# First two tiles behind a layer norm computed from the un-normalised input

## The chip, the cores and the metric

One core of a Trainium2 chip runs the whole program. The metric is device time in microseconds from start to end of one execution, the median of three.

## What is computed

Two model blocks at T = 512 tokens and D = 1024. The second block is, in order: sparse attention, layer norm, gated feed-forward, layer norm, HGRN mixer, layer norm, gated feed-forward, layer norm. What the change touches is this:

```python
for layer in range(2):
    mix = dsa_mixer(h, ...) if layer == 0 else hgrn2_mixer(h, ...)
    h = layer_norm(ALPHA * h + mix, ln_g[layer, 0], ln_b[layer, 0])
    ffn = (silu(h @ w_gate[layer]) * (h @ w_up[layer])) @ w_down[layer]
    h = layer_norm(ALPHA * h + ffn, ln_g[layer, 1], ln_b[layer, 1])

def layer_norm(x, g, b):        # mean and variance over the 1024 features of a token
    return (x - mu) * rsqrt(var + 1e-5) * g + b
```

Three of these norms are followed by a matrix product on their result: behind the attention's output projection (`wo`) comes the first feed-forward (`ffn0`), behind `ffn0` comes the HGRN stage, behind HGRN's output projection (`ho`) comes `ffn1`. The fourth norm is stored.

## The kernel before

Activations lie transposed: 128 features on the partitions, 512 tokens along the free axis, eight such tiles (KT = 8) in `c.x`. Weights stream from HBM as slabs of 128 x 1024 numbers, each slab holding the eight 128 x 128 blocks (k = 0 to 7) of one output tile, into a ring of four buffers. float32 precision is kept by splitting each number into a high part (type fp32r) and the rest: ACT casts a slab (`cast_slab`, L145), DVE subtracts (`split_slab`, L150), and each product of a weight block with an activation tile is three matmuls (`product`, L176 to L178) of 128x128 weights and 512 columns. An output tile is therefore 24 matmuls in one PSUM bank. Two slabs (three in the HGRN stage) are held split at a time; PE waits for the split, ACT's next cast waits for PE to be done with the slab that it replaces. All ordering is by semaphores written by hand; within an engine the program order holds.

The program is a list of stages with a barrier of all engines between them. At a boundary with a layer norm this happens:

- `stage_project` (L1879) or the second half of `stage_ffn` (L2003) makes output tile m = 0 to 7. DVE adds it to the residual in `c.x` (L1935 or L2137), ACT squares it (`scalar_square`, L1730), and DVE and POOL keep running sums of x and of its squares over tiles 0 to 6 (L1747, L1738).
- When the last product is done, `Norm.tensor` (L1750) sums over the partitions on PE with single-column matmuls (L1758): the running sums first, then tile 7 and its square. DVE and ACT make mean, variance and the inverse root (`Norm.vector` L1790, `Norm.scalar` L1781), PE spreads the two resulting rows over all partitions (L1777) into banks 2 and 3. Between the sums and the spread PE runs `warm` (L184), matmuls whose results nobody reads. Meanwhile ACT casts and DVE splits three slabs of the next stage. Then the stage ends.
- In the next stage `Apply` normalises in place: for each k DVE multiplies and adds (L1831, L1834), ACT makes the high part with g and b (L1845) and the full value (L1847), POOL subtracts (L1853). PE runs `warm` again (ten calls) and then `first_pair` (L209): output tiles 0 and 1 advance together, k by k, each k as `Apply` delivers it. Then tiles 2 and 3, then the loop.

In the feed-forward stage the slabs alternate gate and up; four slabs are a turn. ACT applies Silu to the gate tile (L2081), DVE multiplies by the up tile (L2115), both parts of the result go to `hid` (L2084, L2118). In the HGRN stage (L2660) four slabs make one head (forget gate, value, query, output gate, tiles u = 4h to 4h+3), computed in banks 0 and 1 in turn; ACT's `taken` (L2845) moves each tile out of its bank. PE runs `dense(4)`, `turned(0)` (transposes of head 0 through banks 2 and 3), `dense(5)`, `inner(0)`, `update(0)`, `dense(6)`, `outer(0)` (L2781), and so on.

Of the kernel before, what the change touches and what calls it, by code (L numbers as in the profile page):

```python
# [13 lines left out]
P = 128  # L14
# [53 lines left out]
class Ctx:  # L68
# [58 lines left out]
    def place_third(self, n, tile):  # L127

        at = self.bigr[:, tile:tile + 4, :].rearrange("p a b -> p (a b)")
        self.third = {n: at.rearrange("p (a k c) -> p a k c", a=2, k=KT)}  # L130
# [9 lines left out]
    def cast_slab(self, act, n, i=0):  # L140

        act.wait_ge(self.slab_ready[n % RING], 16 * (n // RING + 1) + i * 16)
        if n >= self.held and n not in self.third:
            act.wait_ge(self.slab_done, n - self.held + 1 + i * RING)
        act.activation(self.place(n)[:, 0, :, :], self.ring[:, n % RING, :, :], ACT.Copy).then_inc(self.slab_cast, 1)  # L145
# [1566 lines left out]

class Norm:
# [4 lines left out]
    def __init__(self, c, tag, squares, at, kind, g, b=None, eps=1):  # L1718
        self.squares = squares
# [7 lines left out]

    def scalar_square(self, act, added, m):
        wait_tile(act, added, m)
        act.activation(self.squares[:, m, :], self.c.x[:, m, :], ACT.Square).then_inc(self.sq_out, 1)  # L1730

    def pool(self, pool):

        for m in range(1, KT - 1):
            pool.wait_ge(self.sq_out, m + 1)
            if m > 1:
                pool.wait_ge(self.sq_added, m - 1)
            pool.tensor_tensor(self.acc[:, 1, :], self.squares[:, 0, :] if m == 1 else self.acc[:, 1, :],  # L1738
                               self.squares[:, m, :], ALU.add).then_inc(self.sq_added, 1)
# [10 lines left out]
    def tensor(self, pe, added):  # L1750

        c = self.c
        one = con(c, "ones")[:, 0:1]

        def sums(bank, x, first):
            for q in range(QT):
                for half in HALVES:
                    mm = pe.matmul(bank[half, q:q + 1], x[:, q * P:(q + 1) * P][:, half], one, start=first and q == 0,  # L1758
                                   stop=not first, skip_group_check=True)
            return mm  # L1760

        wait_tile(pe, added, KT - 3)
        if self.kind == "ln":
            pe.wait_ge(self.x_added, KT - 2)
            sums(c.bank[0], self.acc[:, 0, :], True)
        pe.wait_ge(self.sq_added, KT - 2)
        sums(c.bank[1], self.acc[:, 1, :], True)
        if self.kind == "ln":
            pe.wait_ge(added, KT)
            sums(c.bank[0], c.x[:, KT - 1, :], False).then_inc(self.sums, 1)  # L1770
        pe.wait_ge(self.sq_out, KT)
        sums(c.bank[1], self.squares[:, KT - 1, :], False).then_inc(self.sums, 1)
        warm(c, pe, c.bank[4], 4)
        pe.wait_ge(self.small, 1)
        for j, row in enumerate((4, 5)[:2 if self.kind == "ln" else 1]):
            for q in range(QT):
                mm = pe.matmul(c.bank[2 + j][:, q * P:(q + 1) * P], self.st[:, row, q:q + 1].to_broadcast([P, P]),  # L1777
# [3 lines left out]
    def scalar(self, act, ahead=None):  # L1781
# [4 lines left out]
        if ahead:  # L1786
# [3 lines left out]
    def vector(self, dve, ahead=None):  # L1790
# [3 lines left out]
        if self.kind == "ln":  # L1794
            ch.link(dve.tensor_scalar(st[:, 0, :], c.bank[0][:, 0:QT], 1.0 / D, None, ALU.mult))
            ch.link(dve.tensor_tensor(st[:, 1, :], st[:, 0, :], st[:, 0, :], ALU.mult))
            dve.wait_ge(self.sums, 2)
            dve.scalar_tensor_tensor(st[:, 2, :], c.bank[1][:, 0:QT], 1.0 / D, st[:, 1, :], ALU.mult, ALU.subtract)\
               .then_inc(self.root, 1)
        else:  # L1800
            dve.tensor_scalar(st[:, 2, :], c.bank[1][:, 0:QT], 1.0 / D, None, ALU.mult).then_inc(self.root, 1)
# [6 lines left out]
        if ahead:  # L1808
# [4 lines left out]
class Apply:  # L1813
# [3 lines left out]
    def __init__(self, c, tag, parts=True):  # L1817
        self.c, self.n, self.parts = c, c.norm, parts
# [3 lines left out]
    def vector(self, dve):  # L1822
# [6 lines left out]
        for k in range(KT + 1):  # L1829
            if k < KT:  # L1830
                dve.tensor_tensor(c.x[:, k, :], c.x[:, k, :], c.bank[2][:, :], ALU.mult).then_inc(self.scaled, 1)  # L1831
            if k >= 1:
                dve.wait_ge(self.scaled, k)
                dve.tensor_tensor(c.x[:, k - 1, :], c.x[:, k - 1, :], c.bank[3][:, :], ALU.add).then_inc(self.normed, 1)  # L1834

    def scalar(self, act):
        c, n = self.c, self.n
        for k in range(KT):
# [5 lines left out]
            if self.parts:  # L1844
                act.activation(c.hr[:, k, :], c.x[:, k, :], ACT.Identity, **affine).then_inc(self.cast, 1)  # L1845
# [25 lines left out]
FFN_THIRD, DSA_THIRD = 20, 24  # L1871
# [7 lines left out]
def stage_project(c, tag, slab, alpha, norm, next_parts, src=None, begun=0, parts=(1,)):  # L1879
# [3 lines left out]
    norm = Norm(c, tag, c.big, 10, *norm)  # L1883
    c.place_parts(*parts)
    c.norm = norm
    yp = parts_of(c, f"{tag}_y", c.y if src is None else src)

    def after():

        c.place_parts(*next_parts(c))  # L1890
        c.place_third(slab + KT + 2, FFN_THIRD)
        return slab + KT

    with nc.Block() as block:
# [17 lines left out]
        def _(act):  # L1912
# [3 lines left out]
            for m in range(KT):  # L1916
                if m + PARTS < KT:
                    c.cast_slab(act, slab + m + PARTS)
                norm.scalar_square(act, added, m)
            norm.scalar(act, after())  # L1920
            c.place_parts(*parts)
# [6 lines left out]
        def _(dve):  # L1928
            if not begun:
                open_dense(c, yp, slab, dve=dve)  # L1930
            for m in range(KT):
                if m + PARTS < KT:
                    c.split_slab(dve, slab + m + PARTS)
# [6 lines left out]
def stage_out(c):  # L1940
# [9 lines left out]
    def next_stage():  # L1950

        c.place_parts(*dsa_parts(c))
        c.place_third(slab + slabs + 2, DSA_THIRD)
# [49 lines left out]
def stage_ffn(c, layer):  # L2003
# [6 lines left out]
    xp = Apply(c, f"{tag}x")  # L2010
    norm = Norm(c, tag, c.h, 27, "ln", ("ln_g", (2 * layer + 1) * KT), ("ln_b2", (2 * layer + 1) * KT))
# [3 lines left out]
    c.place_parts(*ffn_parts(c))  # L2015
    c.norm = norm
    down_made = c.sem(f"{tag}_down_made")
# [11 lines left out]
    with nc.Block() as block:  # L2029
# [6 lines left out]
        def _(pe):  # L2036

            def gate_up(u, i):
                c.slab_wait(pe, gu + u, i)
                for k in range(KT):  # L2040
                    mm = product(pe, c.bank[u][:, :], c.slab_parts(gu + u, k), xp.tile(k), k == 0, k == KT - 1)
                mm.then_inc(c.slab_done, 1)

            c.place_third(gu + 2, FFN_THIRD)
# [5 lines left out]
            c.third = {}  # L2050
# [7 lines left out]
            for n in range(KT * FT):  # L2058
# [3 lines left out]
                if m == 0:  # L2062
                    pe.wait_ge(hidden_out, j + 1)
                mm = product(pe, down_bank(m), c.slab_parts(dn + n // KT, n % KT), (hid[:, j, :], hid_lo[:, j, :]),
# [8 lines left out]
        def _(act):  # L2073
            def turn(i, first):

                for u in range(2):
                    c.slab_done_wait(act, gu + 2 * u, i)
                    if u or not first:
                        c.cast_slab(act, gu + 2 * u + PARTS, i)
# [3 lines left out]
                    act.wait_ge(prod_out, i * 2 + (u + 1))  # L2083
                    act.activation(hid[:, i * 2 + u, :], prod[:, u, :], ACT.Copy).then_inc(cast_out, 1)  # L2084
# [3 lines left out]
            turn(0, True)  # L2088
            with act.Fori(1, FT // 2) as i:
                turn(i, False)  # L2090
            act.preload_act_table(ACT.Sqrt)
            for s in range(FT):
                if s + PARTS < FT:
                    c.cast_slab(act, dn + s + PARTS)
                if s in down_end:
                    norm.scalar_square(act, added, down_end.index(s))
            norm.scalar(act, after())
            c.place_parts(*ffn_parts(c))
# [7 lines left out]
        def _(dve):  # L2106
            def turn(i, first):

                for u in range(2):
                    for v in range(2):  # L2110
                        if u or v or not first:
                            c.split_slab(dve, gu + 2 * u + v + PARTS, i)
# [3 lines left out]

                    dve.wait_ge(cast_out, i * 2 + (u + 1))
                    dve.tensor_tensor(hid_lo[:, i * 2 + u, :], prod[:, u, :], hid[:, i * 2 + u, :].bitcast(F32), ALU.subtract)\  # L2118
                       .then_inc(hidden_out, 1)

            xp.vector(dve)
            turn(0, True)
            with dve.Fori(1, FT // 2) as i:
                turn(i, False)
            made = 0
            for s in range(FT):
                if s + PARTS < FT:
                    c.split_slab(dve, dn + s + PARTS)
                if s in down_end:

                    m = down_end.index(s)
# [1129 lines left out]
```

## Time and profile before

| | us |
|---|---|
| median of 3 runs | 1902.44 |
| lowest, highest | 1901.03, 1903.01 |
| the profiled execution | 1900.69 |
| its span, first to last instruction | 1898.8 |
| PE busy | 1811.3 (95%) |
| DVE busy | 897.9 (47%) |
| ACT busy | 781.5 (41%) |
| POOL busy | 246.2 (13%) |
| mean granted TensorE clock | 0.985 |

The page has the busy time of each engine over the whole span and in 40 slices, the granted TensorE clock in the same slices, and the groups of instructions by line. A busy PE is not always a useful one: L184 (`warm`) counts as busy. The four boundaries with a layer norm lie near 818, 1192, 1503 and 1878 us of the span; the first three are those that the change touches.

### The profile page before, as it was taken

What the parts mean: (1) busy time and instruction counts of PE and PEld (TensorE: products, weight loads), DVE (VectorE), ACT (ScalarE), POOL (GpSimd) and SP (SyncE); (2) the same over time, 40 slices, a digit from 0 to 9 for tenths busy, and PEclk for the clock granted to TensorE, in tenths of its full rate; (3) what the DMA queues carried; (4) which work ended last, traced back from release to release, by engine and by line L of the source; (5) the groups of instructions that cost most, each with busy time, mean ns of one, the idle gap of its engine ahead of it and who ended that gap; (6) DMA issues with size and microseconds to landing.
All of it is one profiled execution on the core that took longest, in us unless ns stands there. A gap on an engine that the chain in (4) does not pass through costs nothing. (4 is left out here: it accounts for less than half of the span.)

```text
span 1898.8 us, 31549 instructions
## 1 busy us (share of the span) xinstructions
PE 1811.3 (95%) x12642; PEld 1419.9 (75%) x12642; DVE 897.9 (47%) x1644; ACT 781.5 (41%) x1341; POOL 246.2 (13%) x205
## 2 busy tenths in 40 slices
PE   6999999899899899999999999999998999999996
PEld 5776666576775666778888888788887778888885
DVE  2673554555557796343333323654554533333223
ACT  4543444455443445342323222765563333222222
POOL 3011232000125000120000000322320210000000
PEclk9999999899999899999999999999999999999998
DMA  5231101200121000213323233222221222332331
GB/s 185 89 92 66 35 25 36 84 23 12 45 74 45 1 1 1 75 64 95 99 99 91 97 100 98 66 87 69 77 67 31 92 75 91 99 99 94 95 100 45
DMA packets 38488, 134.00 MB, mean 71 GB/s; under 512 B 4896, under 2 KB 5344, under 8 KB 38112
## 3 DMA queue, kind: packets, MB, share of 16 engines
q1 hardware_dynamic: 37504, 130.07, 21.5%
q8 instruction: 87, 1.43, 0.3%
q10 hardware_dynamic: 864, 2.23, 0.3%
q14 instruction: 33, 0.27, 0.0%
HBM read 129.40 MB, written 2.10 MB: 69 GB/s over the span
## 5 line engine op out<-in xcount | busy, mean ns | idle before, releaser
L150 DVE TENSOR_TENSOR big_parts<-ring,big_parts 128x1024 fp32r<-128x1024 f32 x181 | 226.7, 1256 | 532.6 <-ACT big_parts L145 531.2
L176 PE MATMUL bank<-h_parts,big_parts 128*128 128x512 f32 (+1 forms) x1072 | 423.9, 395 | 8.3 <-DVE big_parts L150 4.9
L177 PE MATMUL bank<-y_parts,big_parts 128*128 128x512 f32 (+1 forms) x1072 | 417.2, 389 | 0.0
L178 PE MATMUL bank<-h_parts,big_parts 128*128 128x512 f32 (+1 forms) x1072 | 417.2, 389 | 0.0
L145 ACT ACTIVATE big_parts<-ring 128x1024 fp32r<-128x1024 f32 x181 | 191.3, 1060 | 382.9 <-PE bank L178 380.1
L176 PEld LDWEIGHTS bank<-h_parts,big_parts 128*128 128x128 f32 x1072 | 201.9, 188 | 59.0 <-POOL y_parts L1853 6.8
L178 PEld LDWEIGHTS bank<-h_parts,big_parts 128*128 128x128 f32 x1072 | 201.8, 188 | 42.0
L177 PEld LDWEIGHTS bank<-y_parts,big_parts 128*128 128x128 f32 x1072 | 202.0, 188 | 39.4
L176 PE MATMUL bank<-big_parts 128*128 128x512 f32 x352 | 136.9, 389 | 0.0
L177 PE MATMUL bank<-work_parts,big_parts 128*128 128x512 f32 x352 | 136.9, 389 | 0.0
L178 PE MATMUL bank<-big_parts 128*128 128x512 f32 x352 | 136.9, 389 | 0.0
L1235 ACT ACTIVATE work<-work 128x256 f32<-128x256 f32 (+4 forms) x128 | 67.1, 524 | 110.9 <-DVE work L1257 110.5
L184 PE MATMUL bank<-cst 128*128 128x256 f32 x356 | 101.1, 413 | 8.2 <-PEq L92 8.2
L176 PE MATMUL bank<-h_parts,work_parts 128*128 128x512 f32 x232 | 93.9, 405 | 1.2 <-PEq L92 0.8
L184 PEld LDWEIGHTS bank<-cst 128*128 128x128 f32 x356 | 70.8, 207 | 28.1 <-issue 15.5
L1257 DVE CUSTOM_DVE_ANT_0 work<-bank,big 128x256 f32<-128x256 f32 (+4 forms) x128 | 56.8, 444 | 73.2 <-PE bank L1204 63.7
L178 PE MATMUL bank<-h_parts,work_parts 128*128 128x512 f32 x232 | 90.5, 390 | 0.0
L177 PE MATMUL bank<-y_parts,work_parts 128*128 128x512 f32 x232 | 90.4, 390 | 0.0
L832 PE MATMUL bank<-x,ring 128*128 128x512 f32 x176 | 85.7, 610 | 0.2 <-ACT big L1031 0.2
L150 DVE TENSOR_TENSOR work_parts<-ring,work_parts 128x1024 fp32r<-128x1024 f32 x37 | 46.2, 1252 | 76.9 <-ACT work_parts L145 76.8
L177 PEld LDWEIGHTS bank<-work_parts,big_parts 128*128 128x128 f32 x352 | 66.1, 188 | 13.8
L176 PEld LDWEIGHTS bank<-big_parts 128*128 128x128 f32 x352 | 66.1, 188 | 13.7
(399 smaller groups left out, 2696.1 us busy)
## 6 DMA issues: line engine op xcount, KB each, us to landing
ring<-in_wstream SPq DMA_DIRECT2D x229, 512.0 KB, 3.6
x<-in_xt SPq DMA_DIRECT2D x8, 512.0 KB, 6.7
out_t<-x SPq DMA_DIRECT2D x8, 256.0 KB, 2.0
work<-in_memt ACTq DMA_DIRECT2D x1, 1024.0 KB, 14.2
y<-in_cw SPq DMA_DIRECT2D x1, 1024.0 KB, 5.0
cst<-in_cst ACTq DMA_DIRECT2D x1, 768.0 KB, 7.9
cos<-in_reset SPq DMA_DIRECT2D x2, 256.0 KB, 6.8
big<-work SPq DMA_DIRECT2D x4, 128.0 KB, 4.5
```

What stands on the lines that cost most here:

```text
L145: act.activation(self.place(n)[:, 0, :, :], self.ring[:, n % RING, :, :], ACT.Copy).then_inc(self.slab_cast, 1)
L150: dve.tensor_tensor(self.place(n)[:, 1, :, :], self.ring[:, n % RING, :, :], self.place(n)[:, 0, :, :].bitcast(F32), ALU.subtract).then_in ...
L176: pe.matmul(out, w[0], x[0], start=start, stop=False, skip_group_check=True)
L177: pe.matmul(out, w[0], x[1], start=False, stop=False, skip_group_check=True)
L178: return pe.matmul(out, w[1], x[0], start=False, stop=stop, skip_group_check=True)
L184: pe.matmul(bank[:, 0:2 * P], con(c, "ident"), c.cst[:, 0:2, :], start=True, stop=True)
L832: mm = pe.matmul(c.bank[DENSE_BANK][:, :], c.raw_slab(n, k), c.x[:, k, :], start=k == 0, stop=k == KT - 1)
L1235: act.activation(e, e, ACT.Exp, bias=self.low[:, n:n + 1], scale=-1.0, accum_out=self.den[:, n:n + 1])\
L1257: dve.tensor_tensor_reduce(self.weights(n), self.c.bank[self.SCORES[n % 3]][:, 0:u.keys], u.mask, -self.scale, 3e38, ALU.add, ALU.min, sel ...
```

## The change

At the first three boundaries output tiles 0 and 1 of the next stage no longer wait for the norm. With W a weight block and r, mu the inverse deviation and mean of a token, W(g(x - mu)r + b) = r W(gx) - (mu r) W g + W b. A new class `Raw` holds g times x in two parts, made tile by tile while the stage before still runs. PE multiplies with these; the two vectors W g and W b come from 16 small matmuls on the unsplit slabs in the ring (two columns each). k = 0 and 1 of both tiles are done among the statistics, k = 2 to 7 at the start of the next stage (`raw_products`). Then ACT copies both banks out (`copy_opened`) after its whole share of `Apply`, and DVE multiplies by r and adds (`open_tile`); W b goes in as a bias of the first use. Tile 2 now runs alone, k by k with `Apply`.

What moves with it: the running sums are reduced before the last product (last two k-steps in `ffn0`) rather than behind it (`early`); all `warm` calls at these boundaries go; the slabs of tiles 0 and 1 are cast and split inside the loop over m, to places of their own, and behind the norm only two slabs are (tiles 2 and 3); sums and spread use other banks. In HGRN tiles 2 and 3 use banks 2 and 3, so `turned(0)` waits for tile_out 4 instead of 2, the slab of tile 4 is split behind `open_tile`, and `decays` comes behind that. In `ffn0` the squares have two buffers instead of eight.

```diff
+class Raw:
+    def scalar(self, act, k):
+        act.activation(self.hi[:, k, :], self.c.x[:, k, :], ACT.Copy, scale=vec(self.c, self.g[0], self.g[1] + k)).then_inc(self.cast, 1)
+    def vector(self, dve, k):
+        dve.wait_ge(self.cast, k + 1)
+        dve.scalar_tensor_tensor(self.lo[:, k, :], self.c.x[:, k, :], vec(...), self.hi[:, k, :].bitcast(F32), ALU.mult, ALU.subtract)...
+    def columns(self, pe):
+        for u in range(2):
+            c.raw_wait(pe, self.slab + u)
+            for k in range(KT):
+                mm = pe.matmul(c.bank[2][:, 2 * u:2 * u + 2], c.raw_slab(self.slab + u, k), c.vecs[:, g:b + 1:b - g], ...)
+        mm.then_inc(self.cols_made, 1)
+    def begin(self, pe, k):
+        pe.wait_ge(self.split, k + 1)
+        if k == 0:
+            for u in range(2):
+                self.c.slab_wait(pe, self.slab + u)
+        self.product(pe, k)
...
     def scalar_square(self, act, added, m):
...
+        if self.raw:
+            self.raw.scalar(act, m)
...
     def tensor(self, pe, added):
+        if self.raw:
+            self.raw.begin(pe, 0)
+        else:
+            self.early(pe, added)
         if self.kind == "ln":
             pe.wait_ge(added, KT)
...
-        warm(c, pe, c.bank[4], 4)
+        if self.raw:
+            for k in range(1, Raw.BEGUN):
+                self.raw.begin(pe, k)
+        else:
+            warm(c, pe, c.bank[4], 4)
         pe.wait_ge(self.small, 1)
...
         ins.then_inc(self.small, 1)
-        if ahead:
+        if self.raw:
+            self.raw.vector(dve, KT - 1)
+            self.raw.columns_out(dve)
+            for n in range(2, 4):
+                c.split_slab(dve, ahead + n)
...
+    def open_tile(self, dve, u):
+        dve.wait_ge(self.opened_raw, u + 1)
+        dve.tensor_tensor(self.opened[u], self.opened[u], n.spread_banks[0][:, :], ALU.mult).then_inc(self.opened_half, 1)
+        dve.wait_ge(self.opened_half, u + 1)
+        dve.scalar_tensor_tensor(self.opened[u], n.spread_banks[1][:, :], self.raw.columns_at[:, 2 * u:2 * u + 1], self.opened[u],
+                                 ALU.mult, ALU.add).then_inc(self.opened_out, 1)
...
 stage_project, tensor:
+                    if m == KT - 1 and k == KT - 1:
+                        norm.early(pe, added)
...
 stage_ffn, tensor:
-            warm(c, pe, c.bank[4], 10)
-            first_pair(c, pe, gu, xp)
-            xp.wait_banks(pe)
-            for u in range(2, 4):
-                gate_up(u, 0)
+            xp.raw_products(pe)
+            onward()
+            gate_up(2, 0, True)
+            gate_up(3, 0)
...
 stage_ffn, scalar:
             xp.scalar(act)
-            turn(0, True)
+            xp.copy_opened(act)
+            xp.opened_wait(act, 0)
+            act.activation(silu[:, 0, :], xp.opened[0], ACT.Silu, bias=xp.opened_bias(0)).then_inc(silu_out, 1)
+            high(0, 0)
+            turn(0, (1,))
...
 stage_hgrn, tensor:
-                pe.wait_ge(tile_out, 4 * h + 2)
+                pe.wait_ge(tile_out, 4 * h + 2 if h else 4)
...
 stage_hgrn, scalar and vector:
             xp.scalar(act)
+            xp.copy_opened(act)
+            c.cast_slab(act, n0 + 4)
...
             xp.vector(dve)
+            for u in range(2):
+                xp.open_tile(dve, u)
+            c.split_slab(dve, n0 + 4)
             decays()
```

## Rows read from the trace of the kernel before

**Rows 1.** Page: busy us, share of the span and instructions by engine.

```profile
PE 1811.3 (95%) x12642; PEld 1419.9 (75%) x12642; DVE 897.9 (47%) x1644; ACT 781.5 (41%) x1341; POOL 246.2 (13%) x205
```

**Rows 2.** Timeline, PE, first boundary: start us, length us, instruction, idle before.

```profile
818.49 1.10 PE L1758 MATMUL bank<-cst,work 128*64 128x1 f32 x32
819.45 0.61 PE L1758 MATMUL bank<-cst,x 128*64 128x1 f32 x16
820.01 0.63 PE L1758 MATMUL bank<-cst,big 128*64 128x1 f32 x16
820.57 3.06 PE L184 MATMUL bank<-cst 128*128 128x256 f32 x8
823.43 2.58 PE L1777 MATMUL bank<-cst,work 128*128 128x128 f32 x16
826.80 4.56 PE L184 MATMUL bank<-cst 128*128 128x256 f32 x20 [0.79 <-PEq L92]
831.88 0.47 PE L176 MATMUL bank<-h_parts,big_parts 128*128 128x512 f32 x1 [0.52 <-POOL y_parts L1853]
```

**Rows 3.** Timeline, DVE, the same stretch.

```profile
818.60 0.69 DVE L1935 SCALAR_TENSOR_TENSOR x<-x,bank 128x512 f32<-128x512 f32 x1 [4.02 <-PE bank L178]
...
821.50 0.16 DVE L1806 SCALAR_TENSOR_TENSOR work<-work 128x4 f32<-128x4 f32 x1
822.23 3.50 DVE L150 TENSOR_TENSOR big_parts<-ring,big_parts 128x1024 fp32r<-128x1024 f32 x3 [0.57 <-ACT big_parts L145]
```

**Rows 4.** Timeline, ACT, the same stretch.

```profile
829.57 0.82 ACT L1847 ACTIVATE x<-x,vecs 128x512 f32<-128x512 f32 x1
...
831.13 0.81 ACT L1847 ACTIVATE x<-x,vecs 128x512 f32<-128x512 f32 x1
```

**Rows 5.** Window: length, busy of PE to POOL, granted clock, DMA, GB/s.

```profile
822.00:823.00 1.00, 1.00 (x3) 0.73 (x3) 0.77 (x1) 1.00 (x2) 0.00 (x0) 0.50 0.00 0
```

**Rows 6.** Timeline, PE: third gate-up tile, first tile of the loop.

```profile
844.21 0.39 PE L176 MATMUL bank<-h_parts,big_parts 128*128 128x512 f32 x1
...
855.10 0.39 PE L176 MATMUL bank<-h_parts,big_parts 128*128 128x512 f32 x1
```

**Rows 7.** Timeline, PE, second boundary and the first head of the HGRN stage.

```profile
1192.47 1.10 PE L1758 MATMUL bank<-cst,work 128*64 128x1 f32 x32
...
1194.55 1.99 PE L184 MATMUL bank<-cst 128*128 128x256 f32 x8
1196.38 1.95 PE L1777 MATMUL bank<-cst,work 128*128 128x128 f32 x16
...
1200.55 4.55 PE L184 MATMUL bank<-cst 128*128 128x256 f32 x20 [2.22 <-PEq L92]
...
1236.70 0.48 PE L176 MATMUL bank<-h_parts,big_parts 128*128 128x512 f32 x1
...
1251.30 1.05 PE L2789 MATMUL bank<-work 128*128 128x128 f32 x8
```

**Rows 8.** Timeline, PE, third boundary.

```profile
1503.30 1.10 PE L1758 MATMUL bank<-cst,work 128*64 128x1 f32 x32
...
1511.31 4.55 PE L184 MATMUL bank<-cst 128*128 128x256 f32 x20 [2.16 <-PEq L92]
```

**Rows 9.** Timeline, ACT, first head of the HGRN stage.

```profile
1216.35 0.22 ACT L2864 ACTIVATE work<-work 128x16 f32<-128x16 f32 x1
1216.58 1.28 ACT L2848 ACT_TABLE_LOAD   x1
...
1218.37 1.05 ACT L145 ACTIVATE big_parts<-ring 128x1024 fp32r<-128x1024 f32 x1
...
1231.04 0.59 ACT L2848 ACTIVATE big<-bank 128x512 f32<-128x512 f32 x1
```

**Rows 10.** Timeline, PE, start of the second project stage.

```profile
1467.92 0.79 PE L176 MATMUL bank<-h_parts,big_parts 128*128 128x512 f32 x1 [4.87 <-DVE big_parts L150]
...
1473.21 0.43 PE L176 MATMUL bank<-h_parts,big_parts 128*128 128x512 f32 x1
```

More of the change, by code:

```diff
@@ L125, in place_parts, with place_apart @@
         self.third = {}
-    def place_third(self, n, tile):
-        at = self.bigr[:, tile:tile + 4, :].rearrange("p a b -> p (a b)")
-        self.third = {n: at.rearrange("p (a k c) -> p a k c", a=2, k=KT)}
+    def place_apart(self, tiles):
+        self.third = {n: self.bigr[:, tile:tile + 4, :].rearrange("p a b -> p (a b)").rearrange("p (a k c) -> p a k c", a=2, k=KT)
+                      for n, tile in tiles.items()}
     def place(self, n):
@@ L1726, in __init__, with square @@
         self.st = wk(c, 0, 8, QT)
+    def square(self, m):
+        return self.squares[:, m % self.squares.shape[1], :]
     def scalar_square(self, act, added, m):
         wait_tile(act, added, m)
-        act.activation(self.squares[:, m, :], self.c.x[:, m, :], ACT.Square).then_inc(self.sq_out, 1)
+        held = self.squares.shape[1]
+        if m >= held:
+            act.wait_ge(self.sq_added, max(1, m - held))
+        act.activation(self.square(m), self.c.x[:, m, :], ACT.Square).then_inc(self.sq_out, 1)
+        if self.raw:
+            self.raw.scalar(act, m)
     def pool(self, pool):
@@ L1748, in vector_add, with column_sums, early @@
                               ALU.add).then_inc(self.x_added, 1)
[L1750 to L1760, printed above, removed]
+    def column_sums(self, pe, bank, x, first):
+        for q in range(QT):
+            for half in HALVES:
+                mm = pe.matmul(bank[half, q:q + 1], x[:, q * P:(q + 1) * P][:, half], con(self.c, "ones")[:, 0:1],
+                               start=first and q == 0, stop=not first, skip_group_check=True)
+        return mm
+    def early(self, pe, added):
         wait_tile(pe, added, KT - 3)
@@ L1807, in vector @@
         ins.then_inc(self.small, 1)
-        if ahead:
+        if self.raw:
+            self.raw.vector(dve, KT - 1)
+            self.raw.columns_out(dve)
+            for n in range(2, 4):
+                c.split_slab(dve, ahead + n)
+        elif ahead:
             for n in range(3):
@@ L1882, in stage_project, with here @@
     added = c.sem(f"{tag}_added")
-    norm = Norm(c, tag, c.big, 10, *norm)
-    c.place_parts(*parts)
+    ahead = slab + KT
+    raw = Raw(c, tag, ahead, *norm[1:], wkr(c, T, KT, T), wkr(c, 12 * T, KT, T))
+    norm = Norm(c, tag, c.big, 10, *norm, raw=raw)
     c.norm = norm
+    def here():
+        c.place_parts(*parts)
+        c.place_apart({ahead: FFN_APART[0], ahead + 1: FFN_APART[1]})
+    here()
     yp = parts_of(c, f"{tag}_y", c.y if src is None else src)
@@ L1890, in after @@
         c.place_parts(*next_parts(c))
-        c.place_third(slab + KT + 2, FFN_THIRD)
-        return slab + KT
+        return ahead
     with nc.Block() as block:
@@ L2063, in _ @@
                     pe.wait_ge(hidden_out, j + 1)
+                if raw and m == KT - 1 and j == FT - 2:
+                    norm.early(pe, added)
                 mm = product(pe, down_bank(m), c.slab_parts(dn + n // KT, n % KT), (hid[:, j, :], hid_lo[:, j, :]),
@@ L2106, in _, with low, turn @@
         def _(dve):
-            def turn(i, first):
-                for u in range(2):
+            def low(i, u):
+                dve.wait_ge(cast_out, i * 2 + (u + 1))
+                dve.tensor_tensor(hid_lo[:, i * 2 + u, :], prod[:, u, :], hid[:, i * 2 + u, :].bitcast(F32), ALU.subtract)\
+                   .then_inc(hidden_out, 1)
+            def turn(i, us):
+                for u in us:
                     for v in range(2):
-                        if u or v or not first:
-                            c.split_slab(dve, gu + 2 * u + v + PARTS, i)
+                        c.split_slab(dve, gu + 2 * u + v + PARTS, i)
                     dve.wait_ge(silu_out, i * 2 + (u + 1))
@@ L2953, in split @@
             def split(u):
-                if u < ahead:
+                if 4 < u < ahead:
                     c.split_slab(dve, n0 + u)
@@ L3041, in _ @@
             xp.vector(dve)
+            for u in range(2):
+                xp.open_tile(dve, u)
+            c.split_slab(dve, n0 + 4)
             decays()
```

194 lines of the change are left out of this document (137 added, 57 removed).

## The prediction, as recorded before the run

> **What bounds the kernel now.** I read the page first: PE is busy 95% of the span, every other engine under half [rows 1]. So the time is PE's, and a change counts by the PE time it takes out, plus any gap it opens. Then the timeline of PE around a layer norm, because the busy share hides something there. The first boundary's last product is done at 818.49 and the next product starts at 831.88 [rows 2]. In these 13.4 us PE does 2.1 us of single-column sums and 2.6 us of spreading; the two L184 rows, 3.06 and 4.56 us, are work that nobody reads. The reader is to see that PE is "busy" and waits for DVE, ACT and POOL. The DVE timeline shows the chain: last addition 0.11 us after the last product, the small statistics done at 821.66 (L1806), three splits until 825.73, barrier, next stage at 826.80 [rows 2, 3]. There PE waits 5.08 us for the first k of `Apply`; from then on ACT sets the pace, two activations in 1.56 us per k (829.57 to 831.13) [rows 4]. A pair of tiles needs 6 matmuls per k. Two whole tiles, 48 matmuls, go from 844.21 to 855.10: 0.227 us each, 5.44 us a tile [rows 6], so a k of the pair is 1.36 us of work in a 1.56 us slot.
>
> All times below are full clock first. E is the end of the last product before the norm, S the start of the next stage, E' and S' the same after the change.
>
> **From the last product to the next stage.** *Moved ahead of E:* the reduction of the running sums, 0.96 us (819.45 - 818.49) [rows 2]. Before, DVE's addition of tile 7 hid it; now it lies bare on PE. *Added ahead of E:* 16 matmuls of 128x128 float32 weights and two columns. The trace has no such shape. Lower bound: the sums with 64-wide weights and one column, 0.96 / 32 = 0.030 us, doubled for the width, 1.0 us in all. Upper bound: the spread's 128x128 weights with 128 columns, 16 in 1.95 us at full clock [rows 7]. I take 1.9, since its weight block is the same and a load of weights does not shrink with the columns. So E' = E + 2.9 (2.0 to 2.9).
>
> *Behind E':* k = 0 of two tiles, six matmuls, 1.36 us, covers the addition. Then sums of tile 7 and its square, 0.56 us each (820.01 - 819.45) [rows 2]: the last begins at 1.92. From the start of that group to the end of L1806 it was 1.65 us (821.66 - 820.01) [rows 2, 3], so the statistics are there at E' + 3.57. PE does k = 1 until 3.84 and the spread in at most 2.58 [rows 2]: 6.4. DVE has the low part of g x tile 7 (0.69, as L1935), a small copy (0.16) and two splits of 3.50 / 3 = 1.17 us [rows 3]: E' + 6.85 with the small gaps. DVE stays the last, and the barrier adds 0.84 (the smallest gap in these rows is 0.79 [rows 2]): S' = E' + 7.7. Before, S - E was 8.31, 8.08 and 8.01 us at the three boundaries [rows 2, 7, 8]. With 2.9 before E', S' is later than S by 2.3, 2.5 and 2.6 us. One split fewer on DVE is about eaten by k = 0 ahead of the sums and the two DVE steps.
>
> The additional work inside the loop over m (ACT's g x, 0.6 to 0.8 us per tile; DVE's low part 0.69) I cost at nothing: a tile gives 5.44 us, ACT then has about 2.5 and DVE about 3.1 us of work in it. If that cover went, PE would wait for the split of slab m + 2; the smallest margin I find is 1.5 us, at the second tile of the `wo` stage. The squares' two buffers cost nothing either: POOL needs 1.3 us and tiles are 15 us apart there.
>
> **The feed-forward stages (two).** Before: the loop's first tile starts 28.3 us behind S (855.10 - 826.80) [rows 2, 6]. After: k = 2 to 7 of the pair, 36 matmuls, 8.2 us, need nothing. Tile 2 can start k at S' + 5.08 + 1.556 k, the last at 15.97 (+ 0.6 of doubt), and three matmuls take 0.68: its end is S' + 16.6. Tile 3 ends at S' + 22.05. Gain within the stage 6.25 us; what is late next is `Apply`, tile 2 has 5.44 us of work in the 8.4 that are left. Net 6.25 - 2.3 = 3.95 and 6.25 - 2.6 = 3.65. The new end of the pair does not bind: ACT ends `Apply` at S' + 14.5, copies two banks (1.1), DVE opens both tiles (4 x 0.65) by 17.8, the first product of gate and up and its parts are there at 20, the slab of the loop's first tile is split at 21.5, 0.5 us before PE asks for it. That is thin; each us that ACT is later is a us of PE.
>
> **The HGRN stage.** It is different, because ACT moves every tile. Before, ACT takes tile 3 at 1231.04 (ends 1231.63), S + 31.1, and its Exp for the gate bounds runs at S + 15.8 [rows 7, 9]. After: copies until S' + 15.6, DVE opens until 17.8, splits slab 4 until 18.9, begins `decays`, and ACT's Exp comes at 19.4: 3.6 us later. From there the chain keeps its table loads (1.28 each) and loses two casts (1.05 each) and half a us of waiting [rows 9]: tile 3 is out at S' + 32.4. `turned(0)` now wants just that. PE is done with `dense(4)` at S' + 27.5 and stands 4.9 us. `dense(5)` starts at S' + 33.2, before at S + 36.15 [rows 7]; with S' = S + 2.5 that is 0.5 us gained. Head 0's states on DVE hold `outer(0)` at S' + 48.1; before it ran at S + 50.75 = S' + 48.2 [rows 7]. So this boundary gives nothing: 0.1 us.
>
> **The clock.** After 2.1 us of single-column sums at the first boundary the granted clock was 0.50, the lower of the two levels (1.2 instead of 2.4 GHz), and eight L184 matmuls took 3.06 instead of 1.99 us [rows 2, 5, 7]; at the second boundary the same sums did no harm. It was hidden behind DVE. After the change the stretch of narrow matmuls is 2.9 us and what follows, k = 0, leads to the sums, on the path. Bounds: 0, or 1.36 us (k = 0 at half rate) and a little more, up to 1.7. I take 1.3 at two boundaries of three: 2.6. The gap of 4.9 us in HGRN has a twin: at 1467.92 PE had stood 4.87 us, and the matmuls from there to 1473.21 came at half rate [rows 10], 5.3 us for 2.65 of work. Price 0 to 2.6; I take 1.5, of which 0.5 hides behind head 0's states: 1.0.
>
> The Trainium skill, "TensorE: Matmul & The Clock Gate", section "Why this matters for your kernels", speaks against removing filler matmuls: it says to keep the engine continuously busy and that gaps between bursts send it back to the slow clock. By it all four places would pay and tile 2, at 44% duty, might too; that is the rival "slower".
>
> **Sum.** 3.95 + 3.65 + 0.1 - 1.0 - 2.6 = 4.1 us. Against the profiled execution's own 1900.69 (span 1898.8 and 1.9 around it) that gives 1896.6; the median of the runs is 1.75 above that execution, so 1898.3.
>
> **The rivals.**
> - *The clock holds.* Single-column sums cost no clock at two of three boundaries, so it may hold. Then 7.6 us less: 1894.8; with the columns at their lower bound 2.7 more, 1892.1. Against it: the narrow stretch is longer than the one behind which it fell.
> - *ACT's chain is the bound.* The change doesn't do what it says where ACT is last: openings and copies come after all of `Apply`. If ACT and DVE are 1 us later than summed at each boundary (margin 0.5 in the feed-forward, none in HGRN), 2.5 us go: 1901, no change that can be told.
> - *Slower: the clock falls wherever PE is thinned.* In tile 2's stretch each k is 0.68 us in 1.56. At half rate a k still fits (1.36), but tile 3 behind it doubles. At 2.65 us a place [rows 10], the seven places (three norms, three tiles 2, one gap) cost 18.5 against the 7.7 gained: 1913. It decides from three such places on. For it: rows 5 and 10. Against it: the pair's other stretches are full.
>
> **How the numbers follow.** Forecast 0.45 (own range 1896 to 1901), clock holds 0.25, ACT's chain 0.18, slower 0.12. The range 1893 to 1904.5 leaves out the far ends of the first and last rival. 0.2% is 3.8 us, about what a measurement of this kernel can tell; faster means under 1898.6. That is all of "clock holds" and a bit over half of the forecast: 0.50; slower by as much 0.11; within 0.39.
>
> **What would show it.** Columns: the new group's 16 matmuls last 1.0 or 1.9 us. S' - E' near 7.7. First tile of the feed-forward loop at S' + 22, `dense(5)` at S' + 33, PE's longest wait there for ACT, near 4.9 us. Granted clock 0.5 in a few us behind E'. Wrong would be: PE waiting for a split at the loop's start, a wait for `added` in the loop over m, or half clock in tile 3.

## The result and the profile after

The changed kernel is slower. Six runs of each on one chip:

| | before | after |
|---|---|---|
| median, us | 1902.31 | 1908.66 |
| lowest, highest | 1901.03, 1905.36 | 1907.88, 1910.73 |
| ratio, 95% interval | | 1.0036 [1.0026, 1.0046] |
| span of the profiled execution | 1898.8 | 1906.7 |
| mean granted clock | 0.985 | 0.976 |

From the page of after, busy time by engine, the line that answers to [rows 1]:

```profile
PE 1814.9 (95%) x12654; PEld 1424.9 (75%) x12654; DVE 919.3 (48%) x1683; ACT 798.9 (42%) x1371; POOL 245.1 (13%) x205
```

The difference is a third of a per cent, but the interval lies clear of 1. Two executions further down, far slower than the others of the same kernel (2268 us for the last one, 5389 for before), are left out of the medians.

PE is no less busy than before, although all filler matmuls at three boundaries are gone.

Timeline of PE in after, first boundary (start us, length us, instruction, idle before), which answers to [rows 2]:

```profile
819.77 1.10 PE L1810 MATMUL bank<-cst,work 128*64 128x1 f32 x32
820.80 4.92 PE L1738 MATMUL bank<-vecs,ring 128*128 128x2 f32 x32
825.59 0.77 PE L176 MATMUL bank<-h_parts,work_parts 128*128 128x512 f32 x1
...
827.01 0.63 PE L176 MATMUL bank<-work_parts,big_parts 128*128 128x512 f32 x1
...
835.73 0.47 PE L176 MATMUL bank<-work_parts,big_parts 128*128 128x512 f32 x1 [1.47 <-PEq L92]
```

The early sums (L1810) and the columns (L1738) stand ahead of the last product, which begins at 825.59. At 827.01 starts k = 0 of the new pair (the place that the prediction calls E'), and the next stage starts at 835.73 (S'). The same rows at the other two boundaries answer to [rows 7, 8]:

```profile
1193.89 1.10 PE L1810 MATMUL bank<-cst,work 128*64 128x1 f32 x32
1194.92 3.73 PE L1738 MATMUL bank<-vecs,ring 128*128 128x2 f32 x32
1198.51 0.73 PE L176 MATMUL bank<-big_parts 128*128 128x512 f32 x1
...
1201.17 0.63 PE L176 MATMUL bank<-y_parts,big_parts 128*128 128x512 f32 x1
...
1209.07 0.47 PE L176 MATMUL bank<-y_parts,big_parts 128*128 128x512 f32 x1 [1.57 <-PEq L92]
...
1508.51 1.10 PE L1810 MATMUL bank<-cst,work 128*64 128x1 f32 x32
1509.54 4.24 PE L1738 MATMUL bank<-vecs,ring 128*128 128x2 f32 x32
1513.64 0.77 PE L176 MATMUL bank<-h_parts,big_parts 128*128 128x512 f32 x1
...
1515.07 0.63 PE L176 MATMUL bank<-work_parts,big_parts 128*128 128x512 f32 x1
...
1525.31 0.47 PE L176 MATMUL bank<-work_parts,big_parts 128*128 128x512 f32 x1 [0.81 <-PEq L92]
```

Two things are to be seen. The columns are 32 instructions, not 16, and take 3.7 us or more. And a matmul of 512 columns behind them takes 0.63 us instead of 0.39. The windows (length, busy of PE to POOL, granted clock, DMA, GB/s), which answer to [rows 5], say why:

```profile
820.00:825.00 5.00, 5.00 (x60) 4.98 (x58) 1.89 (x2) 0.31 (x1) 0.11 (x1) 0.81 0.01 3
825.00:828.00 3.00, 3.00 (x10) 2.52 (x10) 0.69 (x1) 0.03 (x1) 0.00 (x0) 0.50 0.00 0
1198.00:1202.00 4.00, 4.00 (x14) 3.25 (x15) 0.59 (x1) 0.00 (x0) 0.00 (x0) 0.57 0.00 0
1516.00:1520.00 4.00, 4.00 (x38) 3.14 (x37) 0.49 (x3) 1.29 (x3) 0.00 (x0) 0.50 0.02 4
844.00:852.00 8.00, 6.15 (x24) 3.84 (x23) 2.61 (x5) 7.05 (x10) 6.45 (x5) 1.00 0.00 0
```

At all three boundaries the clock is at its lower level (0.50, 1.2 GHz) where the path runs, though at the second only for about 3 us. The last row is tile 2's stretch in step with `Apply` at the first boundary: there the clock held, as it did in the same stretch behind the other two (1.00 in the windows 1217 to 1225 and 1534 to 1542).

### The profile page after: what moved, and what is told of

It reads as the page before. It is cut to its first block and busy times, and to the rows that moved or that the text cites. A ratio compares the mean times of both kernels' runs of the same rounds, so it can differ in the third digit from the quotient of the medians.

```text
span 1906.7 us, 31644 instructions
## 1 busy us (share of the span) xinstructions
PE 1814.9 (95%) x12654; PEld 1424.9 (75%) x12654; DVE 919.3 (48%) x1683; ACT 798.9 (42%) x1371; POOL 245.1 (13%) x205
## 3 DMA queue, kind: packets, MB, share of 16 engines
q8 instruction: 87, 1.43, 0.3%
## 5 line engine op out<-in xcount | busy, mean ns | idle before, releaser
L176 PE MATMUL bank<-h_parts,big_parts 128*128 128x512 f32 (+1 forms) x1024 | 404.6, 395 | 11.4 <-POOL y_parts L1972 5.3
L177 PE MATMUL bank<-y_parts,big_parts 128*128 128x512 f32 (+1 forms) x1024 | 398.9, 390 | 0.0
L178 PE MATMUL bank<-h_parts,big_parts 128*128 128x512 f32 (+1 forms) x1024 | 398.7, 389 | 0.0
L176 PEld LDWEIGHTS bank<-h_parts,big_parts 128*128 128x128 f32 x1024 | 193.3, 189 | 57.1 <-POOL y_parts L1972 10.8
L178 PEld LDWEIGHTS bank<-h_parts,big_parts 128*128 128x128 f32 x1024 | 193.1, 189 | 40.2
L177 PEld LDWEIGHTS bank<-y_parts,big_parts 128*128 128x128 f32 x1024 | 193.4, 189 | 38.0
L177 PE MATMUL bank<-work_parts,big_parts 128*128 128x512 f32 x384 | 151.3, 394 | 0.0
L1794 POOL TENSOR_TENSOR work<-big 128x512 f32<-128x512 f32 x4 | 5.2, 1296 | 630.8 <-ACT big L1784 630.8
L177 PEld LDWEIGHTS bank<-work_parts,big_parts 128*128 128x128 f32 x384 | 73.2, 191 | 15.2
L184 PE MATMUL bank<-cst 128*128 128x256 f32 x272 | 79.8, 415 | 3.0 <-PEq L92 3.0
```

Source lines behind the costliest of these rows:

```text
L176: pe.matmul(out, w[0], x[0], start=start, stop=False, skip_group_check=True)
L177: pe.matmul(out, w[0], x[1], start=False, stop=False, skip_group_check=True)
L178: return pe.matmul(out, w[1], x[0], start=False, stop=stop, skip_group_check=True)
L184: pe.matmul(bank[:, 0:2 * P], con(c, "ident"), c.cst[:, 0:2, :], start=True, stop=True)
L1794: pool.tensor_tensor(self.acc[:, 1, :], self.square(0) if m == 1 else self.acc[:, 1, :], self.square(m), ALU.add).then_inc(self.sq_added, 1)
```

## The experiments

Theory A, formed on the rows above: the loss is the columns themselves, twice as many instructions as counted, plus the lower clock that they bring. Rival B: it is all clock, and the number of columns matters little. Rival C: it lies elsewhere, in the additional work in the loop over m or in the chain behind the norm. The kernels do not all share a chip: "one k", "given out", "columns alone" and "behind the path" ran on one (before there: 1901.35), "sixteen instructions", "first steps of `decays`" and "`dense(5)`" on another (before there: 1902.04). The ratios are each against before on the same chip; a difference from the changed kernel's 1908.66 crosses chips and is good to about 1 us. Rows and windows come from one profiled execution of each kernel.

**One k of eight columns.**

```diff
     def columns(self, pe):
         for u in range(2):
-            for k in range(KT):
+            for k in range(1):
```

> Two of the sixteen column matmuls stay (k = 0 of both tiles), the other fourteen are left out, so W g and W b are wrong and with them the output. Theory A (the columns' own time on PE: the trace shows 32 instructions of about 0.132 us, 4.24 us a boundary, where the sum had 16 in 1.9): 28 instructions go at each of three boundaries, 3 x 3.7 = 11.1 us, and the clock falls less: 1894 to 1897.5 against 1908.7. Theory B (the fallen clock is the loss, because the filler matmuls are gone, and the columns are only a part of it): at most 5 us less, 1903 or more. Theory C (something else in the added work inside the loop over the tiles): no change.

Measured: 1889.89 (1887.49 to 1893.07), ratio 0.9946 [0.9930, 0.9963]. Timeline of PE at its first boundary, and two windows:

```profile
817.82 1.10 PE L1810 MATMUL bank<-cst,work 128*64 128x1 f32 x32
818.85 0.61 PE L1738 MATMUL bank<-vecs,ring 128*128 128x2 f32 x4
...
818.00:822.00 4.00, 4.00 (x61) 3.35 (x59) 2.58 (x3) 1.35 (x3) 0.17 (x1) 1.00 0.02 4
822.00:826.00 4.00, 4.00 (x45) 3.54 (x42) 3.16 (x9) 2.45 (x4) 0.00 (x0) 1.00 0.00 0
```

Two matmuls of the code are four instructions. The whole loss goes, and more than that: 18.8 us off the changed kernel (17.8 with each kernel taken against before on its own chip), where theory A's range ended at 1894 and B allowed 5 us at most. B and C fall. What was too small in A is the clock's share, since 14 of the 16 matmuls at 3.59 us a boundary (1198.51 - 1194.92) are only 9.4; the expectation's 4.24 was the row of the third boundary, where the clock had begun to fall. This kernel has no filler matmuls at the three boundaries either, and its clock stays full at all three: taking the fillers out does not bring the lower clock by itself.

**The same columns, given out among the last tile's products.** Sixteen float32 matmuls as in the change, one k (four instructions) ahead of each of the last eight k-steps of the last tile (shown for `stage_project`; `stage_ffn` has the same ahead of its last eight).

```diff
+                    if m == KT - 1:
+                        raw.columns(pe, [k])
...
     def early(self, pe, added):
-        if self.raw:
-            self.raw.columns(pe)
```

> The sixteen column matmuls are given out one k at a time between the products of the last tile, so PE has the same work but no stretch of 5 us with narrow matmuls only. Theory A (PE time of the columns): the 12.7 us stay; only what the half clock costs goes, 1.3 to 2.6 us a boundary at most: 1901 to 1906. Theory B (clock is the loss): 1900 or less, and no granted clock of 0.5 within 10 us behind the last product. If giving them out costs weight loads of its own, the time is above 1906 with the clock at full.

Measured: 1898.99 (1896.56 to 1902.80, ten runs), ratio 0.9986 [0.9977, 0.9996]. Timeline of PE around one k at the first boundary, and the windows behind the early sums of each of the three:

```profile
816.63 0.50 PE L1739 MATMUL bank<-vecs,ring 128*128 128x2 f32 x4
816.99 0.47 PE L176 MATMUL bank<-h_parts,work_parts 128*128 128x512 f32 x1
...
817.77 0.50 PE L1739 MATMUL bank<-vecs,ring 128*128 128x2 f32 x4
...
824.00:828.00 4.00, 4.00 (x48) 3.28 (x47) 2.12 (x9) 2.91 (x5) 0.00 (x0) 1.00 0.00 0
1195.00:1199.00 4.00, 4.00 (x46) 3.16 (x45) 1.76 (x7) 2.19 (x4) 0.00 (x0) 1.00 0.01 4
1505.00:1509.00 4.00, 4.00 (x59) 3.27 (x56) 1.16 (x4) 1.25 (x2) 0.00 (x0) 1.00 0.01 4
```

A k takes 1.14 us (817.77 - 816.63) where its three matmuls of 512 columns alone take 0.68: 0.46 more, 3.7 a boundary. So the columns cost PE what they cost in a block, but the clock holds at all three places, and 9.7 us are back (8.7 with each kernel taken against before on its own chip). By its number this run came out as theory B said (1900 or less, full clock), not as A (1901 or more). But B's "the number of columns matters little" falls with the two runs together: they shared a chip, the clock is full at the boundaries in both, and the 28 instructions between them are 9.1 us (9.4 by the rows). So the columns' own time and the clock that their block brings are each about half of the matter.

**The columns alone, in the kernel before.** The same 16 matmuls ahead of the last product at the same three boundaries, their result unused; nothing else of the change.

```diff
+                    if m == KT - 1 and k == KT - 1:
+                        pe.wait_ge(added, KT - 2)
+                        dead_columns(c, pe, slab + KT, norm.g[1])
```

> The kernel before, with the same sixteen column matmuls ahead of the last product at the three boundaries, their result unused. Theory A: their price by itself is 3 x 4.24 = 12.7 us at full clock, plus what the clock loses: 1902.4 + 12.7 = 1915 to 1920. Theory B: the columns alone cost little where the filler matmuls are still there: under 1910.

Measured: 1921.03 (1918.22 to 1923.62), ratio 1.0109 [1.0092, 1.0126]. Timeline of PE at the first boundary, and a window at each of the three:

```profile
818.14 3.63 PE L1719 MATMUL bank<-vecs,ring 128*128 128x2 f32 x32
...
821.00:831.00 10.00, 10.00 (x86) 8.52 (x87) 4.25 (x9) 3.77 (x5) 0.00 (x0) 0.54 0.01 2
1201.00:1214.00 13.00, 13.00 (x94) 11.23 (x95) 5.01 (x9) 3.77 (x5) 0.00 (x0) 0.50 0.01 1
1521.00:1528.00 7.00, 7.00 (x75) 6.27 (x76) 3.92 (x9) 3.77 (x5) 0.00 (x0) 0.53 0.00 0
```

The columns alone make the kernel before 19.7 us slower, just above theory A's 1915 to 1920; B (under 1910) falls. From the start of the columns to the start of the next stage the three places take 15.6, 18.0 and 14.1 us in this timeline, against 9.0, 9.4 and 8.7 for the same stretch without them (S less the start of the last product, from [rows 2, 7, 8]): 20.6 more. Of that 11.7 are the columns' own group, and the windows show the rest as time at half clock. All the filler matmuls are in this kernel, and the clock falls at three places instead of one. The columns are then more than the whole loss, and the rest of the change is a gain, as forecast.

**Sixteen instructions at the change's place.** The columns take the slabs' high parts and copies of g and b in fp32r, so that a matmul is one instruction (W g and W b are then taken from the high parts of W, g and b alone).

```diff
-            c.raw_wait(pe, self.slab + u)
+            c.slab_wait(pe, self.slab + u)
             for k in range(KT):
-                mm = pe.matmul(..., c.raw_slab(self.slab + u, k), c.vecs[:, g:b + 1:b - g],
+                mm = pe.matmul(..., c.slab_parts(self.slab + u, k)[0], c.colr[:, :, k],
```

> The columns stay where the change put them, ahead of the last product, but are made from the high parts in fp32r: 16 instructions instead of 32, the number that the prediction's sum had. Theory A (the sum failed only by the count of instructions and by the clock that the longer stretch cost): the stretch ahead of the last product is near 2.9 us and the time is what the prediction said, 1898.3, or up to 3 us below it if the clock holds (1895 to 1899). Theory D (the rest of the sum was wrong too, the narrow stretch costs whatever its length): 1903 or more.

Measured: 1898.17 (1897.20 to 1903.40, ten runs), ratio 0.9985 [0.9975, 0.9995]. Timeline of PE at the second boundary, then the windows behind the columns at the first, second and third:

```profile
1189.98 1.10 PE L1818 MATMUL bank<-cst,work 128*64 128x1 f32 x32
1191.01 1.95 PE L1746 MATMUL bank<-colr,big_parts 128*128 128x2 f32 x16
1192.82 0.48 PE L176 MATMUL bank<-big_parts 128*128 128x512 f32 x1
...
1194.27 0.39 PE L176 MATMUL bank<-y_parts,big_parts 128*128 128x512 f32 x1
...
1201.75 0.47 PE L176 MATMUL bank<-y_parts,big_parts 128*128 128x512 f32 x1 [1.56 <-PEq L92]
...
822.00:826.00 4.00, 4.00 (x18) 2.78 (x19) 0.69 (x1) 1.24 (x2) 0.00 (x0) 0.59 0.00 0
1192.00:1196.00 4.00, 4.00 (x31) 3.25 (x30) 0.69 (x1) 0.81 (x2) 0.00 (x0) 1.00 0.00 0
1508.00:1512.00 4.00, 4.00 (x26) 3.40 (x27) 2.85 (x9) 2.19 (x3) 0.00 (x0) 0.50 0.00 0
```

With the count that the sum had assumed, the group lasts 1.95 us (forecast 1.9), sums and columns 2.84 (forecast 2.9), E' to S' 7.48 where the clock holds (forecast 7.7), the clock falls at two boundaries of three (as forecast), and the kernel takes 1898.2 (forecast 1898.3), 3.9 under before on its chip where the forecast gain was 4.1. Some of that agreement is luck: the clock's price was still too low. From the early sums to S' this kernel takes 12.56 us at the first boundary (819.29 to 831.85) and 13.41 at the third (1501.26 to 1514.67), against 11.09 at full clock (the second's 11.77 less 0.68 for its second k-step): 1.5 and 2.3 us, not 1.3 each. The price of one instruction was right; their number was not. Operand type and count changed together here; that the price per instruction is the same in both types (1.95 / 16 and 3.73 / 32) is what lets the count be named.

**The columns behind the path.** The same short columns moved into the next stage, where PE waits for `Apply` anyway (ahead of tile 2's k = 4 and 5).

```diff
+    def between(self, pe, k):
+        if k in (4, 5):
+            self.raw.columns(pe, self.held, range(4 * (k - 4), 4 * (k - 3)), self.cols_made)
+        self.wait(pe, k)
```

> The changed kernel with the columns made from the high parts of the two slabs only (fp32r, 16 instructions instead of 32) and moved into the next stage, in the waits of tile 2 for the apply step (ahead of k = 4 and k = 5). Nothing narrow but the sums is left ahead of the last product. Theory A: 4.24 us a boundary go, hidden where PE waits 0.88 us per k anyway: 1908.7 - 12.7 - clock 1 to 4 = 1892 to 1896, faster than before. Theory B: the clock falls all the same behind the bare sums, 1900 or more.

Measured: 1891.40 (1889.38 to 1893.60), ratio 0.9952 [0.9936, 0.9969]. Timeline of PE in the HGRN stage:

```profile
1197.07 0.47 PE L176 MATMUL bank<-y_parts,big_parts 128*128 128x512 f32 x1 [1.50 <-PEq L92]
...
1208.05 0.95 PE L1743 MATMUL bank<-colr,big_parts 128*128 128x2 f32 x8
1209.66 0.95 PE L1743 MATMUL bank<-colr,big_parts 128*128 128x2 f32 x8
...
1229.64 1.12 PE L2930 MATMUL bank<-cst,big 128*128 128x128 f32 x4 [4.81 <-ACT big L3035]
...
1246.52 1.05 PE L2974 MATMUL bank<-work 128*128 128x128 f32 x8
```

Both groups lie in waits that were there: the last k of tile 2 starts 15.9 us behind S' with and without them. The clock is full at all three boundaries, so the early sums alone (1.1 us) do not bring it down. The stand of 4.8 us before `turned(0)` is as the sum had it, and `outer(0)` comes 49.4 us behind the stage's start.

**The first steps of `decays` ahead of the opening.** On top of that kernel, so that ACT's Exp need not wait behind DVE's opening of two tiles and a split.

```diff
             xp.vector(dve)
+            decays()
             for u in range(2):
                 xp.open_tile(dve, u)
             c.split_slab(dve, n0 + 4)
-            decays()
+            decays_rest()
```

> v1_late_columns, and in the HGRN stage the first three small steps of decays on DVE go ahead of the opening of the two tiles, so that ACT's Exp no longer waits for it (1.87 us idle there in v1). If that chain sets the 4.8 us in which PE stands before turned(0), the stand shrinks to about 3.2 us and the time to 1889 or 1890 (v1: 1891.4), a little less again if the clock stays up. If the chain runs elsewhere: as v1.

Measured: 1887.47 (1884.42 to 1888.88), ratio 0.9919 [0.9906, 0.9932]: the best of all. Timeline of PE in the HGRN stage:

```profile
1197.23 0.47 PE L176 MATMUL bank<-y_parts,big_parts 128*128 128x512 f32 x1 [1.50 <-PEq L92]
...
1227.96 0.66 PE L2930 MATMUL bank<-cst,big 128*128 128x128 f32 x4 [2.98 <-ACT big L3035]
...
1245.03 1.05 PE L2974 MATMUL bank<-work 128*128 128x128 f32 x8
```

The stand shrinks from 4.81 to 2.98 us, and `outer(0)` comes 47.8 us behind S', 1.65 earlier. So ACT's chain was what was late, by the order of steps on DVE. The medians of the kernel without this step and of this one differ by 3.9 us, more than these rows give; they come from two chips, and what the rest is stays open.

**`dense(5)` ahead of `turned(0)` for head 0.** On top of the last kernel, to fill the stand that is left.

```diff
+                if s == 1:
+                    dense(4 * s + 1)
                 if s >= 1:
                     turned(s - 1)
-                if 1 <= s < HG:
+                if 1 < s < HG:
                     dense(4 * s + 1)
```

> v2, and in the HGRN stage PE does dense(5) ahead of turned(0) for head 0, so that it has work while ACT empties banks 2 and 3. The stand of 3 to 5 us before turned(0) becomes a stand of about 0.5 us before dense(5), no half clock there; then head 0's keys and states on DVE and ACT hold inner(0) and outer(0), which gives back a part: 1 to 3 us under v2, 1886 to 1889. If head 0's states are all that counts, as v2.

Measured: 1888.92 (1887.37 to 1889.69), ratio 0.9930 [0.9917, 0.9943], no better than without it; the intervals overlap. Timeline of PE in the HGRN stage (the stage starts at 1196.49), and a window:

```profile
1225.11 0.50 PE L176 MATMUL bank<-h_parts,big_parts 128*128 128x512 f32 x1 [0.87 <-DVE big_parts L150]
...
1244.20 1.13 PE L2974 MATMUL bank<-work 128*128 128x128 f32 x8 [2.96 <-issue]
...
1246.00:1249.00 3.00, 3.00 (x20) 2.40 (x17) 1.10 (x2) 0.60 (x1) 0.00 (x0) 0.50 0.39 131
```

The stand is gone at `turned(0)` and is back, 2.96 us long, before `outer(0)`, which comes 47.7 us behind the start, as without the new order (47.8). So PE's order only chooses where to wait, and the half clock moves with it. That the chain of head 0 on ACT and DVE is the floor fits, since moving its steps did move `outer(0)` in the last kernel; the row itself names no releaser ("issue"), and no run shows which step of the chain is last.

## Why the prediction was wrong, step by step

It said 1898.3 us and faster; it is 1908.66 and slower, beyond the range's upper end of 1904.5.

Sum over the three boundaries, from the start of the early sums to S' (after's rows above; forecast at full clock):

| us | forecast | first | second | third |
|---|---|---|---|---|
| early sums and columns | 2.9 | 5.82 | 4.62 | 5.13 |
| last products | 0.68, 1.36, 0.68 | 1.42 | 2.66 | 1.43 |
| E' to S' | 7.7 | 8.72 | 7.90 | 10.24 |
| together | 11.3, 12.0, 11.3 | 15.96 | 15.18 | 16.80 |

Forecast 34.5 and 2.6 for the clock, 37.1; measured 47.9.

- **Wrong: "16 matmuls".** The code has 16, PE executes 32. The price of one was well taken from the row of its weight block: 3.73 / 32 = 0.117 us against 1.95 / 16 = 0.122. The failure is in the count: the row's was divided by instructions, then multiplied by matmuls of the code. It was readable in rows already used. The running sums are two calls of eight float32 matmuls in the code (`column_sums`: four groups of 128 tokens, two halves) and stand as x32 in [rows 2]; the spread is eight in the code (`spread_rows`) and x16 in [rows 7]. By the second boundary, where the clock was full while they ran, columns take 3.59 us instead of 1.9, sums 1.03 instead of 0.96: 1.7 a place, 5.2 in all. The bounds 1.0 to 1.9 were bounds for a wrong count, so the range was too narrow too. The lower one also rested on doubling the price of a 64-wide instruction, 0.030 us; with 128-wide weights and two columns it is 0.117, nearly four times.
- **Wrong in size: the clock.** Booked at two places of three with 1.3 each, 2.6. The excess of 10.8 us less 5.2 leaves 5.6 more, so by this sum the clock cost 8.2. By the rows it is 8.9: at full clock the three places would take 12.78, 13.46 and 12.78 us (4.62, the last products at 0.68, 1.36 and 0.68, and 7.48 from the sixteen-instruction kernel), and they took 3.2, 1.7 and 4.0 more. The runs that spread or drop the columns agree. The mechanism named was the right one, narrow matmuls before the path; wrong were the number of places and the price of one. The price was 1.36 us, one k at half rate, but at the first boundary the clock fell inside the columns and stayed down to 829.9, the end of k = 0, and at the third to 1522.8, through k = 0, the sums and k = 1. How often it falls lines up with the length of the narrow stretch: early sums alone, 1.1 us, nowhere (nine places in three kernels); with one k of columns, 1.6 us, nowhere; the kernel before with 2.1 at one of three [rows 2, 5]; the sixteen instructions with 2.8 at two of three; the change with 4.6 and more at all three. That is one profiled execution of each kernel: it shows an order, no threshold.
- **Right: the statistics behind E'.** 7.48 with full clock, forecast 7.7. The extra work in the loop over m cost nothing that shows: the kernel with one k of columns has all of it, and its early sums at the first boundary start at 817.82 us, where the last product starts in before (818.49 - 0.68 = 817.81).
- **Right: the feed-forward stage.** Its loop starts 22.15 us behind S' (forecast 22.05); before, 28.3:

```profile
857.88 0.39 PE L176 MATMUL bank<-h_parts,big_parts 128*128 128x512 f32 x1
```

- **Right in HGRN, a little short.** PE stood 4.75 us before `turned(0)` (forecast 4.9) and the clock fell within that stand (0.59 in the window 1239 to 1242, 0.50 from 1243 to 1246); `outer(0)` came at S' + 50.2 (forecast 48.1 and 1.0 for the clock), 1.1 more:

```profile
1241.58 1.12 PE L2913 MATMUL bank<-cst,big 128*128 128x128 f32 x4 [4.75 <-ACT big L3018]
1243.20 0.78 PE L176 MATMUL bank<-h_parts,big_parts 128*128 128x512 f32 x1
...
1259.31 1.05 PE L2957 MATMUL bank<-work 128*128 128x128 f32 x8
```

So the forecast gain of 4.1 becomes 10.8 + 1.1 - 4.1 = 7.8 us of loss, against 7.9 between the two profiled spans. That the two agree is partly chance. Cut at the start of the last product (of the last two k-steps at the second boundary) in before, at the early sums in after, and at S and S', the 7.9 us are, in order: 2.0 ahead of the first boundary, 7.0 at it, -6.2 in the stage behind it, 5.7 at the second, -2.6 in the HGRN stage and the projection, 8.1 at the third, and -6.1 behind it. The first 2.0 are not the change, as the one-k kernel has none of them (817.82 above); in after's profile the clock also fell near 96 and 157 us, in unchanged code, and in before's it did not. And at the HGRN stage's end the clock fell in before (first row below) and not in after (second row), about 1.5 us the other way. The medians differ by 6.35.

```profile
1439.00:1442.00 3.00, 3.00 (x19) 2.78 (x18) 1.28 (x4) 0.00 (x0) 0.00 (x0) 0.52 0.00 0
...
1447.00:1450.00 3.00, 3.00 (x30) 2.88 (x29) 1.82 (x6) 0.00 (x0) 0.00 (x0) 1.00 0.00 0
```

Of the rivals, "the clock holds" came near what the change can be: with the columns off the path the kernel takes 1891.4, and its figure with the columns at the lower bound was 1892.1. That is near by luck, since the columns are off the path there and not at that bound. "ACT's chain" was right in HGRN as a place (DVE's order alone takes the ratio from 0.9952 to 0.9919, the intervals just apart, and 1.65 us of that are in the rows of `outer(0)`) but not as the reason for the result. "Slower" came true by its outcome and half by its mechanism: the clock fell at all three norms and in the gap, but never in tile 2's stretch, and its price of 2.65 a place fits the mean of the three norms (3.2, 1.7 and 4.0) but not any one. It laid the falls to PE being thinned and the fillers gone, and the runs above show that the block of columns brings them. The doubled count, which no rival had, did the rest.

## What to carry to other kernels

Count instructions as the trace does, not as the code does: a matmul of two float32 operands is two in these traces, and with 128-wide weights and two columns each costs what one with 128 columns costs. Do not put a block of narrow matmuls on the path right before a chain of short steps, as 3.6 us of them were here; give them out between wide ones, or put them into a wait that is there anyway. Where a stand of PE is filled by reordering, look first whether the next wait hangs on the same chain.

## What the runs showed of the hardware that was not expected

- A matmul with 128x128 weights and two columns takes 0.117 us per instruction in float32 (3.73 / 32) and 0.122 in fp32r (1.95 / 16), both about what the row of the spread with 128 columns gives (0.122, 1.95 / 16): between 2 and 128 columns nothing is saved, and weight loads are busy 4.98 of the 5.00 us of the window 820 to 825. The Trainium skill, "TensorE: Matmul & The Clock Gate", section "LDWEIGHTS (loading the stationary operand)", says that a weight load costs by the weights' columns. The equal price at equal weights agrees; the size does not go in proportion, since the sums with 64-wide weights cost 0.032 us an instruction (1.03 / 32), about a quarter and not a half.
- A float32 matmul is two instructions here (16 in the code, x32 in the row). The Trainium skill, "FP8 and Floating Point Precision", section "TensorE Precision Notes", speaks of four passes for true float32. In time the wide rows agree: four float32 matmuls with 256 columns (`warm`, x8) take 1.99 us [rows 7], 0.50 each, where an fp32r matmul of 256 columns would take about 0.11 (an estimate: half of the 0.227 for 512), so about four times. For the columns it is the number of instructions that decided: 3.73 us for 16.
- The clock falls while PE is busy without a gap. In the window 820 to 825 of after PE was busy 5.00 of 5.00 us, weight loads 4.98, and the clock reached its lower level inside it. The same 32 instructions among matmuls of 512 columns kept it up. The Trainium skill, "TensorE: Matmul & The Clock Gate", section "Why this matters for your kernels", names idle gaps between bursts; these rows show the fall without one.
- In tile 2's stretch PE was busy 6.15 of 8.00 us with waits of about 0.6 us (the row 844 to 852) and the clock stayed at 1.00. One long stand is different: PE stood 4.75 us in after and 4.81 and 2.98 in the two kernels with the columns behind the path, and in each the clock was at its lower level in the stand or within 2 us of its end.
